# Hybrid mixers of a ten-stage network: mask copies, first transposes and a halving put at other places

## What is computed

```python
def hybrid_mixer(h, w_in, ..., w_out):
    p = h @ w_in
    za, qb, kb, vb, gb, qc, kcm, vcm, ksl, vsl, kwn, vwn, gc = jnp.split(p, splits, axis=-1)
    y_a = spatial_gating_mixer(za, ...)
    y_b = retention_mixer(qb, kb, vb, gb, ...)
    y_c = nsa_mixer(qc, kcm, vcm, ksl, vsl, kwn, vwn, gc, ...)
    return jnp.concatenate([y_a, y_b, y_c], axis=-1) @ w_out

def nsa_mixer(...):            # 8 query heads in 2 groups, head size 64, blocks of 128 queries
    o_cmp = softmax(q @ k_cmp) @ v_cmp      # keys compressed 32 to 1, at a stride of 16
    o_sel = softmax(q @ k_s, causal) @ v_s  # the 8 selected blocks of 64 are all 8 there are
    o_win = softmax(q @ k_w, causal) @ v_w  # a window of 512, which is the whole sequence
    return g0 * o_cmp + g1 * o_sel + g2 * o_win
```

## Time and profile before

| | |
|---|---|
| median of 3 runs | 3635.72 us (3631.2 to 3644.97) |
| profiled execution | 3632.66 us, span 3630.9 us |
| PE busy | 3446.2 us, 95% |
| PE weight loads | 2742.8 us, 76% |
| DVE busy | 1943.9 us, 54% |
| ACT busy | 1330.0 us, 37% |
| mean granted clock of PE | 0.972 of full |
| HBM traffic | 93 GB/s over the span |

### The profile page before, as it was taken

One profiled execution on the slowest core, in us unless ns is written; L12 is line 12 of the kernel. 1 busy time (PEld: TensorE's weight loads), 2 busy tenths in 40 slices (PEclk: granted clock), 3 DMA queues, 4 the chain that ended last, 5 costly groups with the idle time before them and its releaser, 6 DMA issues.

```text
span 3630.9 us, 47109 instructions
## 1 busy us (share of the span) xinstructions
PE 3446.2 (95%) x20308; PEld 2742.8 (76%) x20308; DVE 1943.9 (54%) x2721; ACT 1330.0 (37%) x1958; POOL 3.6 (0%) x18
## 2 busy tenths in 40 slices
PE   8999896899999999989999999999999999989998
PEld 6888665778887788877578887766788876668886
DVE  5553576456553754343455434565666455766644
ACT  4322454233222423233633322244444233544433
POOL 0000000000000000000000000000000000000000
PEclk9999996899999999999999999999999999999999
DMA  5444330024444332222013223210232231013221
GB/s 185 140 141 149 116 110 21 4 70 143 144 143 139 128 134 99 99 78 76 1 60 102 95 98 121 95 53 24 77 108 94 99 133 59 30 53 99 99 99 58
DMA packets 93087, 342.41 MB, mean 94 GB/s; under 512 B 10320, under 2 KB 10960, under 8 KB 92368
## 3 DMA queue, kind: packets, MB, share of 16 engines
q1 hardware_dynamic: 92880, 339.40, 27.9%
HBM read 337.26 MB, written 2.10 MB: 93 GB/s over the span
## 4 chain that ended last, share of the span: by engine, by line
PE 86%; DVE 7%; ACT 5%; issue 1%; DMA 0%; SPq 0%; DVEq 0%; ACTq 0%
PE ps L755 21%; PE ps L757 20%; PE ps L756 20%; PE ps L772 3%; PE ps L773 3%; PE ps L776 3%; PE ps L795 1%; PE ps L797 1%; PE ps L796 1%; PE ps L1127 1%; ACT WK L1801 1%; DVE SPL L1894 1%; PE ps L1137 1%; ACT SPH L1366 1%; PE ps L1278 1%
## 5 line engine op out<-in xcount | busy, mean ns | idle before, releaser
L1894 DVE TENSOR_TENSOR SPL<-RAW,SPH 128x1024 fp32r<-128x1024 f32 x522 | 636.7, 1224 | 1067.0 <-ACT SPH L1366 1066.8
L1366 ACT ACTIVATE SPH<-RAW 128x1024 fp32r<-128x1024 f32 x522 | 548.3, 1055 | 1084.3 <-PE ps L757 964.7
L755 PE MATMUL ps<-HH,SPH 128*128 128x512 f32 x2352 | 929.8, 395 | 15.7 <-DVE SPL L1894 6.2
L756 PE MATMUL ps<-HL,SPH 128*128 128x512 f32 x2352 | 918.5, 391 | 0.0
L757 PE MATMUL ps<-HH,SPL 128*128 128x512 f32 x2352 | 918.3, 390 | 0.0
L755 PEld LDWEIGHTS ps<-HH,SPH 128*128 128x128 f32 x2352 | 443.6, 189 | 121.1 <-issue 10.4
L756 PEld LDWEIGHTS ps<-HL,SPH 128*128 128x128 f32 x2352 | 443.6, 189 | 95.3 <-issue 4.1
L757 PEld LDWEIGHTS ps<-HH,SPL 128*128 128x128 f32 x2352 | 443.3, 188 | 93.4
L755 PE MATMUL ps<-AH,SPH 128*128 128x512 f32 x1152 | 449.7, 390 | 0.0
L757 PE MATMUL ps<-AH,SPL 128*128 128x512 f32 x1152 | 448.3, 389 | 0.0
L756 PE MATMUL ps<-AL,SPH 128*128 128x512 f32 x1056 | 410.8, 389 | 0.0
(11 more groups left out here) (430 smaller groups left out, 3576.8 us busy)
## 6 DMA issues: line engine op xcount, KB each, us to landing
RAW<-in_ws SPq DMA_DIRECT2D x522, 512.0 KB, 3.3
RAW<-in_wa SPq DMA_DIRECT2D x96, 512.0 KB, 3.3
WK<-in_sm SPq DMA_DIRECT2D x2, 2784.0 KB, 10.6
WK<-in_cst SPq DMA_DIRECT2D x2, 1664.0 KB, 6.8
X<-in_x SPq DMA_DIRECT2D x8, 256.0 KB, 7.9
out<-X SPq DMA_DIRECT2D x8, 256.0 KB, 2.0
WK<-in_sm SPq DMA_DIRECT2D x1, 768.0 KB, 4.9
PCT<-in_pc SPq DMA_DIRECT2D x1, 349.0 KB, 2.9
```

The lines of the kernel that those rows point to most:

```text
L755: e.matmul(out, wh, rhs[0], start=start, stop=False)
L756: e.matmul(out, wh, rhs[1], start=False, stop=False)
L1366: e.activation(SPH[:, q:q + 1024], RAW[:, r:r + 1024], ACT.Copy).then_inc(hi_ready.did(("hi", n)))
L1894: e.tensor_tensor(SPL[:, q:q + 1024], RAW[:, r:r + 1024], SPH[:, q:q + 1024].bitcast(F32), ALU.subtract).then_inc(lo_ready.did(("lo", n)))
```

## The change

In ACT's program the two copies into CA and IR stand in the loop at tile 13 (`HYB_TILES[13]` is 11), between ACT's copy of that tile and the pieces behind it. CA and IR move to AL 19T to 19T + 256, which is WK 41T to 41T + 256, wholly inside `Gv`. In step 0, PE and ACT take the first two groups of transposes ahead of part 0 of the scores of step 1. The halving up to chunk 23 + AHEAD of the stage (which is 26 and 27, AHEAD being 4) moves: ACT does it behind step 0, DVE in step 1, behind the maxima of the last part and ahead of the copies of the compressed transposes.

```diff
--- before.py
+++ after.py
@@ -407,7 +407,7 @@
                      wsv=H["ws"].rearrange("p (g t) -> p g t", g=4),
                      PTC=[RS[:], ACC[:]], PP=[WK[:, w1 + 2560 * i:w1 + 2560 * i + 2560] for i in range(2)],
                      PT=WK[:, w1 + 5120:w1 + 7680], ST=[SCRX[:, 16 * i:16 * i + 16] for i in range(2)],
-                     CA=AL[:, w1 - NF * T + 7680:w1 - NF * T + 7808], IR=AL[:, w1 - NF * T + 7808:w1 - NF * T + 7936])
+                     CA=AL[:, 19 * T:19 * T + 128], IR=AL[:, 19 * T + 128:19 * T + 256])
             return H
 
         def ahead_of(s, i):
@@ -1332,10 +1332,13 @@
                 scores(0, 2)
                 project(s, 15, wn, cols[15])
                 for m in range(8):
-                    if m < 7:
+
+                    if 0 < m < 7:
                         scores(m + 1, 0)
                     for i in range(5):
                         by_keys(m, i)
+                        if i == 1 and m == 0:
+                            scores(1, 0)
                         if i in (1, 3) and m < 7:
                             scores(m + 1, (i + 1) // 2)
                     if m % 2:
@@ -1782,10 +1785,11 @@
                 for i in range(6, 15):
                     halve_to(BASE[s] + i + 4 + AHEAD)
                     tile(i)
+                    if i == 13:
+                        w.wait_ge(("cmp", s, "v"), ("tables1", s))
+                        e.activation(H["CA"], H["CAUS"], ACT.Copy).then_inc(act_done.did(("ca", s)))
+                        e.activation(H["IR"], IDENT, ACT.Copy).then_inc(act_done.did(("caus", s)))
                     pieces(i)
-                w.wait_ge(("cmp", s, "v"), ("tables1", s))
-                e.activation(H["CA"], H["CAUS"], ACT.Copy).then_inc(act_done.did(("ca", s)))
-                e.activation(H["IR"], IDENT, ACT.Copy).then_inc(act_done.did(("caus", s)))
                 e.preload_act_table_set("exp_and_others")
 
                 qo, ko = [0, 128, 384, 768], [0, 512, 1024, 896]
@@ -1822,14 +1826,17 @@
                 e.activation(H["GT"].rearrange("p (c x) -> p c x", c=4), gsrc, ACT.Tanh, scale=0.5).then_inc(
                     act_done.did(("gtt", s)))
                 scores(0, 2)
-                halve_to(BASE[s] + 23 + AHEAD)
                 for m in range(8):
-                    if m < 7:
+                    if 0 < m < 7:
                         scores(m + 1, 0)
                     for i in range(5):
                         by_keys(m, i)
+                        if i == 1 and m == 0:
+                            scores(1, 0)
                         if i in (1, 3) and m < 7:
                             scores(m + 1, (i + 1) // 2)
+                    if m == 0:
+                        halve_to(BASE[s] + 23 + AHEAD)
                     if 1 <= m <= 4:
                         k = m - 1
                         w.wait_ge(("vp", s, 1, 3), ("sgo", s, k) if k < 2 else ("gnl0", s, k - 2))
@@ -2582,6 +2588,8 @@
                     if m == 0:
                         compressed(0)
                         compressed(1)
+                    elif m == 1:
+                        halve_to(BASE[s] + 23 + AHEAD)
                     if m % 2:
                         r = m // 2
                         for g in range(2):
```

## The result

The changed kernel takes 3628.16 us in the median of 15 runs (3622.88 to 3631.02); the kernel before, run beside it, 3641.12 (3631.2 to 3650.99). The ratio is 0.9968, interval 0.9960 to 0.9975: 11.7 us less (9.1 to 14.6). The forecast was 13.0 less, taken off the one profiled execution of the kernel before (3632.66), so 3620. The median of the kernel before is 8.5 above that execution (one of the 15 runs here was shorter than it), and so the measured time is 8 above the forecast: it lies in the whole range (3611 to 3630), but not in the forecast's own (3616 to 3624). The difference was forecast better than the time.

The account below looks back on a forecast made before the run. PE's work and waits bound the kernel, chiefly its wait for ACT's mask copies, then the halved clock. 10.5 + 1.2 + 2.1 - 0.8 = 13.0 us off 3632.66 gave 3620, own range 3616 to 3624, whole range 3611 to 3630.

Parts of the forecast that it names:

- wait before the first scores: Both hybrid stages: PE's waits of 5.35 and 5.34 us for ACT's mask copies go, less 0.2; 10.5 gained.
- cold work, before less after: Scores and first tokens: half clock still occurs, costing 4.6 us in place of 5.8; gain 1.2, bounds -2 and 5.8.
- wait for the tokens' copies: Tile 15's projection: PE, now earlier, may wait for DVE's last token copy; 0 to 0.7 us per stage, 0 if cold.
- from tile 15 to step 1's transposes: Step 1: transposes ahead of scores and halvings moved away remove PE waits; 1.0 us per stage, bounds 0 and 1.1, together 2.1.
- the halving in step 1: DVE's halving, now in step 1, delays copies and the norm of step 2; costs 0.4 us per stage (0 to 1.2), together 0.8.
- Every link that I had named: First scores: tile 14's copy, score banks, first masking, bank 4 after DVE's second masking; 0.1 us per stage taken for waits.
- Case (a): Rival, both stages: the clock doesn't fall or rises at once, gaining 16.6 us, giving 3616; chance 0.22.
- T0 + 2.5 in place of T0 + 2.9: Step 1: T0 is the end of tile 15's projection, about 2421.0; DVE's maximum starts then without the two halvings before it.
- I take it that DVE's wait for the scores behind it takes that up: Step 2: DVE's next maximum comes 1.3 us late after the moved halving, assumed absorbed by its wait for scores.
- (b): Rival: DVE or ACT holds PE 3 us more in each stage, a new wait replacing the old; 3626, chance 0.15.
- (c): Rival: clock falls in the attention steps, a longer PE wait amid short transposes setting it off; slower, 3654, chance 0.05.
- (d): Rival: the first scores are not freed, something read as early gates them; only 1.3 us gained, 3631, chance 0.05.

Follow-up runs that it names:

- spread_before: Kernel before with only the 64 small matmuls spread, sixteen behind each of four blocks of tile 14's projection; no time given, tile 14 to scores 18.84 us against 15.63.
- block_mid: Changed kernel with all 64 small matmuls as one block between the fourth and fifth weight block of tile 14's projection; no time given, clock fall costs 1.5 us per stage.
- spread_tile: Changed kernel with small matmuls in four groups of sixteen within tile 14's projection, DVE's tile 14 copy ahead of its halving there; ratio 0.9958 (0.9944 to 0.9972).
- half_last: Changed kernel, 32 small matmuls inside tile 14's projection, 32 at the old place, tile 14's copy before DVE's halving, step 1's halving at step 7; ratio 0.9948, median 3621.72.

## Why the prediction was right, point by point

| term | forecast, us | measured in the profile, us |
|---|---|---|
| wait before the first scores | 10.5 | 10.7 |
| cold work, before less after | 1.2 (-2 to 5.8) | -0.4 |
| wait for the tokens' copies | 0 if cold | 0 |
| from tile 15 to step 1's transposes | 2.1 | 2.8 |
| the halving in step 1 | -0.8 | -1.3 |
| sum | 13.0 | 11.8; 12.2 up to step 7 |

The sum is near because the misses are small and partly cancel; that is luck as far as the clock goes, whose term is the difference of a gain in one stage and a loss in the other. The bounds of the terms, added up, are also wider than the "9 to 16" that the prediction gives: their lower ends give some 3, their upper ends some 19. And 3620 itself was taken from one execution, not from a median.

*The first scores.* Right in mechanism and size. Every link that I had named was in time, the tightest (bank 4 for the tokens) by 1.6, because the scores ran cold.

*The clock.* Right that it falls again at the end of the small matmuls although PE doesn't stop; that they are the reason is shown here by the run in the middle of a projection. The size was off: 2.3 per stage was taken, and it was (2.50 - 1.34) + (2.06 - 1.57) = 1.65 in stage one and 1.27 + 1.35 + 2.0 for the tokens = 4.6 in stage two. Before it had been 3.9 and 1.9. So the change gained 2.25 in one stage and lost 2.7 in the other. The lower bound of -2 took that in. Case (a) is out: it would have needed full clock in both stages. A part of its thought may hold for stage one. There the clock was low for 13.6, 13.6 and 10.2 us in the three kernels that keep the wait (before, the halving alone, the transposes alone), and for 3.4 in each of the four profiles of kernels with the copies moved and the small matmuls where they were. In stage two it was 10.2 with the wait, and 10.2 or 6.8 without. What sets these lengths no run here shows.

The rule of the Trainium skill ("TensorE: Matmul & The Clock Gate", "HAM oscillation — how this bites in real kernels"), by which idle gaps make these falls, holds for the kernel whose small matmuls were spread (in "spread_before" full clock until PE had idled 5.0 to 5.3 us), and not for the kernel before or after, where the fall came in work.

*Transposes first.* Right that it gains about 1, wrong in why. I laid the gain to the two halvings that leave DVE's queue. The halving alone gave 0.5 and the transposes alone 1.1: what holds DVE is PE's eight transposes between its two score parts, 0.69 of waiting. The step that failed is "without them the maximum starts when the scores end, T0 + 2.5 in place of T0 + 2.9"; it is true, but worth 0.5 by itself. Both together gave 1.4, more than the bound of 1.1 that I had made from PE's two waits, since the norm was DVE's own chain and not bounded by them.

*The halving one step on.* Right in sign, small in size: 0.4 forecast, 0.67 measured. The step that failed is "I take it that DVE's wait for the scores behind it takes that up". I had looked for the cost at the transposes of step 2, 0.35 for DVE's norm. They gave 0.1 of it: in the kernels with the halving in step 1 they start 0.39 behind the scores' last matmuls and 0.05 behind the end of the norm, in the others 0.28. The rest came another way. The maxima behind the norm came late, so ACT's exponentials did, and so ACT's copy that frees bank 4 for the fourth group of transposes: 0.55 (the row at 2444.23 above). The delay crossed two engines and came back to PE where I had stopped looking; together the two make up the 0.67.

*The rivals.* (b), a new wait of 3 per stage, did not come: PE waits nowhere between L1254 and tile 15. (c) did not come in the changed kernel: its steps 0 to 7 ran at full clock in both stages. Falls in step 7 do occur, in one stage (before, copies, transposes, halving, "spread_before", "block_mid") or both ("spread_tile", "half_last"), with no load under way, and cost 1.5 each, far from the 26 us that would turn the sign. All ten come in the last 0.3 us of PE's wait of 1.80 for the norm of step 7 or in the first 0.8 of the twenty transposes behind it, which in this step alone stand in one run. So the picture of (c), a wait amid transposes, did occur, at a small price; but the changed kernel has the same wait and the same transposes, and no fall, and why is open. What the Trainium skill says of transposes in that page's "Part 4: PE-mode transpose" is not borne out by the changed kernel's steps 0 to 6 either, where transposes stand among the scores; for the run of twenty no run here decides it. (d) is out by the copies alone.

## What to carry to other kernels

An operand that has long been ready and is made in a queue behind something else is a wait that an edit of two lines removes; here, by the profile, it was worth more than all the rest. When the order on one engine is changed, look for the producer's pieces that now follow one another without a gap: scores back to back on PE spared DVE a pause between its maxima, and that was worth more than taking two halvings out of DVE's way. And a delay that is "taken up" by an idle time has to be followed through the engines that are fed by it, until it is back at the one that sets the end.

## What the runs showed of the hardware

The granted clock falls near the end of a dense run of 64 matmuls of 32 columns (3.7 us), with PE not idle before, and in "block_mid" with large matmuls on both sides and no load of weights under way; two runs of 32 (1.9 us each; one kernel), or four of 16 (three kernels), left it at full in both stages. I had expected it from the order of events in the first profile, but not that it would come every time: in the kernels that had the run in one piece, it came in both stages of all eight profiles. Once low it stayed so for 3.4 to 10.2 us of unbroken work, and for up to 13.6 where PE's wait lay in between. The same 64 matmuls cost 3.6 in one run at their old place, 3.8 in two groups and 4.9 in four groups among matmuls of 512 columns. Up to the end of tile 15 the two stages take 70.6 in the changed kernel, 70.1 with four groups and 65.6 with two: four ways lost nearly as much as the clock gave back, and two ways won.
